# One Strassen input stored as f32 sums and split at its use, and low parts moved to VectorE, in a one-core hybrid decoder step

## What is computed

```python
(c_q, c_kv, k_r, z_mla, conv_b, conv_c, conv_h, z_conv,
 q_x, z_x, gates) = split(h @ w_in)                 # w_in: 1024 x (672 + 512*7 + 3072)
y_mla  = latent attention (prompt: causal; sample: 4,096 cached rows in pages)
y_conv = conv_b * conv3(conv_c * conv_h)
y_x    = cross-attention of 4 heads into 256 memory rows
g = sigmoid(gates)
m = (g[0] * ((y_mla  * silu(z_mla))  @ w_p_mla)
   + g[1] * ((y_conv * silu(z_conv)) @ w_p_conv)
   + g[2] * ((y_x    * silu(z_x))    @ w_p_x))
out = layer_norm(2**0.25 * h + m @ w_o)
```

## Time and profile before

| | us |
|---|---|
| runs without profile | 1522.39, 1523.32, 1525.07; median 1523.32 |
| profiled execution | 1521.78 |
| its span, first to last instruction | 1520.0 |
| busy: PE, PEld | 1429.2 (94%), 1238.8 (81%) |
| busy: DVE, ACT, POOL | 845.1 (56%), 521.1 (34%), 304.5 (20%) |
| mean granted TensorE clock | 0.955 of full |

### The profile page before, as it was taken

One profiled execution on the slowest core, in us unless ns is written; L12 is line 12 of the kernel. 1 busy time (PEld: TensorE's weight loads), 2 busy tenths in 40 slices (PEclk: granted clock), 3 DMA queues, 4 the chain that ended last, 5 costly groups with the idle time before them and its releaser, 6 DMA issues.

```text
span 1520.0 us, 28154 instructions
## 1 busy us (share of the span) xinstructions
PE 1429.2 (94%) x11192; PEld 1238.8 (81%) x11192; DVE 845.1 (56%) x1643; ACT 521.1 (34%) x1130; POOL 304.5 (20%) x225
## 2 busy tenths in 40 slices
PE   7997899999988888899899999999999999998997
PEld 7996787777755555556599999999999999998885
DVE  3476347766775334444457577664444444479645
ACT  3331346665361111223333334433333342124100
POOL 3110017666542333330100000000000003236000
PEclk9998899999998777789999999999999999999999
DMA  5465120000472434447912212123333337452522
GB/s 213 126 203 170 54 83 2 1 1 5 130 268 91 133 132 133 161 155 269 380 43 56 85 43 84 45 71 100 101 115 102 100 100 247 158 194 79 223 97 69
DMA packets 117462, 183.29 MB, mean 121 GB/s; under 512 B 14322, under 2 KB 85810, under 8 KB 115540
## 3 DMA queue, kind: packets, MB, share of 16 engines
q1 hardware_dynamic: 107092, 145.84, 29.0%
q0 software_dynamic: 10240, 35.66, 6.9%
HBM read 142.94 MB, written 38.51 MB: 119 GB/s over the span
## 4 chain that ended last, share of the span: by engine, by line
PE 49%; DVE 1%; issue 0%; ACT 0%; DVEq 0%
PE ps L2468 33%; PE ps L2499 10%; PE ps L2533 6%; PE ps L2519 0%; DVE p_ul L2713 0%; DVE p_h L2836 0%; DVE p_h L2839 0%; DVE p_slots L2643 0%; DVE p_stats L2823 0%; DVE p_h L2819 0%; PE ps L2509 0%; DVE p_mv L2830 0%; ACT p_rt L2620 0%; DVE p_rs L2834 0%; DVE p_stats L2828 0%
## 5 line engine op out<-in xcount | busy, mean ns | idle before, releaser
L2468 PE MATMUL ps<-p_x,p_w 128*128 128x272 f32 x4032 | 506.5, 289 | 0.9 <-PEq L2004 0.9
L2468 PEld LDWEIGHTS ps<-p_x,p_w 128*128 128x128 f32 x4032 | 506.3, 188 | 1.0 <-issue 1.0
L1937 POOL TENSOR_TENSOR p_w<-p_wr,p_w 128x512 fp32r<-128x512 f32 x25 | 39.9, 1598 | 645.6 <-ACT p_w L1929 645.6
L1546 PE MATMUL ps<-p_kT,p_q_rows 32*64 32x256 f32 x2048 | 127.5, 503 | 30.2 <-issue 24.6
L2499 PE MATMUL ps<-p_uh,p_w 128*128 128x352 f32 (+1 forms) x576 | 146.4, 334 | 9.0 <-issue 6.2
L1016 POOL TENSOR_SCALAR p_pr<-p_pr,p_rec 128x896 f32<-128x896 f32 (+3 forms) x64 | 109.8, 1725 | 158.6 <-DVE p_rec L980 158.0
L1546 PEld LDWEIGHTS ps<-p_kT,p_q_rows 32*64 32x64 f32 x2048 | 73.1, 172 | 75.9 <-issue 68.4
L2727 DVE TENSOR_TENSOR p_w<-p_sum,p_w 128x512 fp32r<-128x512 f32 x94 | 65.0, 691 | 120.0 <-ACT p_w L1929 120.0
L2499 PEld LDWEIGHTS ps<-p_uh,p_w 128*128 128x128 f32 x576 | 104.6, 193 | 10.7 <-issue 10.7
L1929 ACT ACTIVATE p_w<-p_wr 128x512 fp32r<-128x512 f32 x96 | 60.1, 626 | 141.2 <-PE ps L2499 82.1
L1714 DVE CUSTOM_DVE_ANT_0 p_sc<-ps,p_zero 128x256 f32<-128x256 f32 x64 | 23.4, 421 | 137.9 <-PE ps L1553 87.1
(11 more groups left out here) (338 smaller groups left out, 2584.4 us busy)
## 6 DMA issues: line engine op xcount, KB each, us to landing
p_wr<-w_in SPq DMA_DIRECT2D x48, 512.0 KB, 3.6
g_kept<-p_slots SPq DMA_DIRECT2D x48, 272.0 KB, 2.5
p_x<-t_kept SPq DMA_DIRECT2D x8, 1088.0 KB, 10.0
p_ring<-g_kept SPq DMA_DIRECT2D x16, 544.0 KB, 4.3
p_x<-x_kept SPq DMA_DIRECT2D x6, 1088.0 KB, 7.9
t_kept<-p_t_high SPq DMA_DIRECT2D x16, 272.0 KB, 2.4
t_kept<-p_t_low SPq DMA_DIRECT2D x16, 272.0 KB, 3.1
p_gy<-g_kept SPq DMA_DIRECT2D x8, 544.0 KB, 5.7
```

Of the source, the lines that this page charges most:

```text
L1546: pe.matmul(cols(i, f), q_rows[rows, b % 2, d, :], kT[rows, x:x + S, 2 * f:2 * f + 2, d, :], start=(d == 0), stop=False, tile_position=(32 ...
L2468: last = pe.matmul(ps[:, lo + z, 0:PW], w[:, q % NW, part, t, :], v[:, t, z * PW:(z + 1) * PW], start=(i in STARTS and t == 0 and n == 0), ...
```

## The change

In the first stage the x sums are no longer split. VectorE makes a part in one of eight buffers, and SyncE stores the f32 part once (16 stores instead of 32). Six of the twelve `b_store` calls move into the loop in which x comes in; the other six stand between the later t stores. `high` and `lower` are gone.

The HBM copy of T1 to T4 is one block each, loaded into the place of the low part: ten x loads instead of 14, five of them in decode_attention (B11 twice, T1, T2, B21's high) and five in cross_decode. Two new functions split a block in place: ScalarE copies 128x2176 into the high part (`split_high`), VectorE subtracts (`split_low`). T1 and T2 are split in cross_decode's rounds 4 to 7, T3 and T4 in Strassen group 0.

In the merge, every low part from q = 3 on is made by VectorE, also those of the projections and of w_o. The four `u_low` of branch 0 stand within the last Strassen group. Branches 1 and 2 multiply piece by piece, but add, copy and subtract whole rows of 1,088 columns, in two row buffers.

```diff
-    SETS = 4
+    SETS = 8
...
-        return (n % 2, n // 2) if n < NGR // 2 else (2 + n % 2, (n - NGR // 2) // 2)
+        return (n % 4, n // 4) if n < NGR // 2 else (4 + n % 4, (n - NGR // 2) // 4)
...
+            def t_store(n):
+                z, _ = t_set(n)
+                kt, pp, cols = t_place(n)
+                cols = slice(pp * PW + cols.start, pp * PW + cols.stop)
+                sp.wait_ge(t_step, 4 * (n + 1))
+                sp.dma_start(k["t_kept"][:, :, kt, cols].rearrange("b p w -> p b w"), t_raw[z][:, :, :]
+                             ).then_inc(t_out[z], 16)
...
+                tiles = -((2 * pp + th + 1) * -PW // P)
+                sp.wait_ge((xh_done, xl_done)[part], tiles)
...
+                if 5 <= i < 8:
+                    b_store(4 * (i - 5))
+                    b_store(4 * (i - 5) + 2)
...
+            for n in range(4):
+                t_store(n)
...
+            for n in range(4, NGR // 2):
                 t_store(n)
-                if n - 2 < 12:
-                    b_store(n - 2)
+            for n in range(1, 12, 2):
+                b_store(n)
+                if n >= 5:
+                    t_store((NGR + n - 5) // 2)
+            for n in range(NGR // 2 + 4, NGR):
+                t_store(n)
...
-                    if g < NGR // 2:
-                        high(NGR // 2 + g)
...
-X_EARLY = [(B11, 0), (B11, 1), (T1, 0), (T1, 1), (T2, 0), (T2, 1), (B21, 0), (B21, 1), (T3, 0)]
+X_EARLY = [(B11, 0), (B11, 1), (T1, 1), (T2, 1), (B21, 0)]
+X_PARTS = ((B11, T1, T2), (B21, T3), (B22, T4))
...
+def split_high(nc, act, e, n):
+    blk = T_ORDER[n]
+    hi, lo = e["x"][blk]
+    act.wait_ge(e["x_in"][blk], e["x_all"][blk])
+    nc.scalar.activation(hi[:, :, :], f32(lo[:, :, :]), ACT.Copy).then_inc(e["t_high"], 1)
...
+def split_low(dve, e, n):
+    hi, lo = e["x"][T_ORDER[n]]
+    dve.wait_ge(e["t_high"], n + 1)
+    dve.tensor_tensor(lo[:, :, :], f32(lo[:, :, :]), f32(hi[:, :, :]), ALU.subtract).then_inc(e["t_low"], 1)
...
+                if r in (4, 6):
+                    split_high(nc, act, e, (r - 4) // 2)
...
+                if r in (5, 7):
+                    split_low(dve, e, (r - 5) // 2)
...
+                    if g == 0 and i == 3:
+                        split_high(nc, act, e, 3)
-                    if g == NGRP - 1 and i in (3, 4):
-                        u_high(0, 2 * (i - 3))
-                        u_high(0, 2 * (i - 3) + 1)
+                    if g == NGRP - 1 and i in (2, 3):
+                        u_high(0, 2 * (i - 2))
+                        u_high(0, 2 * (i - 2) + 1)
...
+                    w_o_high(d)
+                    act.wait_ge(zed, d + 1)
+                    nc.scalar.activation(mh[:, d, :], stage[:, d % 2, :], ACT.Copy).then_inc(mh_done, 1)
...
-            for q in (*range(1, NW), *range(NQ1, NQ)):
+            for q in range(1, NW):
                 w_low(nc, pool, e, q)
-                if NQ - 6 <= q < NQ - 2:
-                    for t in range(2):
-                        w_o_low(2 * (q - NQ + 6) + t)
...
+                if g == 0:
+                    split_low(dve, e, 2)
...
                 add(g, 0)
+                if g == 0:
+                    split_low(dve, e, 3)
                 lower(q + A12)
+                if g == NGRP - 1:
+                    u_low(0, 0)
+                    u_low(0, 1)
                 add(g, 1)
                 lower(q + S3)
+                if g == NGRP - 1:
+                    u_low(0, 2)
+                    u_low(0, 3)
...
-            for j in range(4):
-                u_low(0, j)
...
                     dve.tensor_tensor(z, src, gate, ALU.mult).then_inc(freed, 1)
+                    if bi == 2 and n == 0 and d:
+                        m_low(d - 1)
+                if bi:
+                    dve.wait_ge(freed, NP * (p + 1))
+                    dst, z = mt[:, d, :], stage[:, d % 2, :]
                     if bi == 1:
                         dve.tensor_tensor(dst, dst, z, ALU.add).then_inc(summed, 1)
+                    else:
+                        dve.wait_ge(summed, d + 1)
+                        dve.tensor_tensor(z, z, dst, ALU.add).then_inc(zed, 1)
...
+                lower(NQ1 + p + NW)
+                if bi == 2:
+                    w_o_low(d)
+            m_low(KT - 1)
```

More of the change, by code:

```diff
@@ L128, in project_latents @@
     tok, kr = k["tok"], k["kr"]
-    SETS = 4
+    SETS = 8
     size = 4 * 4 * GW
[L132 to L138, removed]
+    places = [at - (4 - z) * size for z in range(4)] + [k["qkv_at"] + z * size for z in range(3)] + [k["w_end"]]
+    t_raw = [Map(nc, where)(f"p1_t_raw{z}", [P, 4, GW]) for z, where in enumerate(places)]
     assert k["qkv_at"] + 3 * size <= w_at + 8 * KT * LAT and k["w_end"] + size <= k["top"] - 4 * 3 * P
@@ L357, in _ @@
                     if h == 1 and n == 0:
-                        for z in range(2):
-                            act.wait_ge(t_out[z], 32 * NGR // 4)
+                        for z in range(4):
+                            act.wait_ge(t_out[z], 32)
                     pn = min(tn, SEQ - t0)
@@ L431, in _ @@
                         make(n)
-                    for n in (2 * (i - 5), 2 * (i - 5) + 1):
-                        lower(n)
             dve.wait_ge(squared, 2 * NT)
@@ L1428, in late_space @@
                   for part in range(2)] for blk in range(7)]
-    first = k["sem"]("p7_x_first")
-    late["x_in"] = {blk: first for blk in X_FIRST} | {blk: k["sem"](f"p7_x_in{blk}") for blk in (T3, B22, T4)}
+    x_in = [k["sem"](f"p7_x_in{z}") for z in range(3)]
+    late["x_in"] = {blk: x_in[z] for z, part in enumerate(X_PARTS) for blk in part}
+    late["x_all"] = {blk: 16 * sum(1 if b in T_ORDER else 2 for b in part) for part in X_PARTS for blk in part}
+    late["t_high"], late["t_low"] = k["sem"]("p7_t_high"), k["sem"]("p7_t_low")
     def x_free(blk, part):
@@ L2205, in merge @@
     raw_o = slabs("p8_raw_o", ring_at[:2], [P, D])
-    stage = Map(nc, e["rest_at"])("p7_stage", [P, ST, PIECES[0][1]])
-    slab_at = [e["rest_at"] + 4 * ST * PIECES[0][1] + 4 * T * d for d in range(5)] + [e["slab_at"]] + ring_at[2:]
+    stage = Map(nc, e["rest_at"])("p7_stage", [P, 2, T])
+    slab_at = [e["rest_at"] + 4 * T * d for d in range(2, 7)] + [e["slab_at"]] + ring_at[2:]
     assert slab_at[4] + 4 * T <= x_at
@@ L2580, in _ @@
             w_high(nc, act, e, 2)
+            split_high(nc, act, e, 2)
             for g in range(NGRP):
@@ L2714, in u_low, with w_o_low, m_low @@
                                   ).then_inc(ul_done, 1)
[L2716 to L2720 removed]
+            def w_o_low(t):
+                dve.wait_ge(oh_done, t + 1)
+                if t == 0:
+                    dve.wait_ge(ul_done, 12)
+                dve.tensor_tensor(ol[t][:, :], raw_o[t % 2][:, :], f32(oh[t][:, :]), ALU.subtract).then_inc(ol_done, 1)
+            def m_low(d):
+                dve.wait_ge(mh_done, d + 1)
+                dve.tensor_tensor(ml[d][:, :], stage[:, d % 2, :], f32(mh[:, d, :]), ALU.subtract).then_inc(ml_done, 1)
             def lower(q):
[L2723 removed]
+                if NW <= q < NQ:
                     dve.wait_ge(w_hi, q + 1)
@@ L2761, in _ @@
                 finish(g, 1)
[L2762 to L2763 removed]
+                if g == NGRP - 1:
+                    lower(q + A22)
             for p in range(NJ):
```

132 lines of the change are left out of this document (33 added, 99 removed).

## The result

The changed kernel took **1484.42 us** (median of 4 runs, 1482.75 to 1488.75) against 1524.19 us for the kernel before, measured beside it (4 runs, 1522.39 to 1525.81). The ratio is 0.9744, 95% interval 0.9719 to 0.9768. The forecast was 1485.6 us, range 1480 to 1495. The profiled execution took 1485.23 us with a span of 1483.4, so the span fell by 36.6 us where the sum said 37.7.

What follows compares the result with a forecast made beforehand. TensorE was taken to set the time almost alone from 751.58 us, with removable waits elsewhere. Terms -20.1 - 1.5 - 2.6 + 0.5 - 6.2 - 7.8 = -37.7 took 1521.78 to 1484.1; 1.5 for the median gave 1485.6 us, range 1480 to 1495.

Steps and rivals of the forecast that it cites:

- First stage: Start to the next stage's first transpose: without splits TensorE no longer waits in the qx loop, ending at 134.0; -20.1 us.
- Clock behind it: Stretch from the next stage's first transpose to the prompt's scores: -1.5 us.
- cross_decode: Fewer loads remove the 5.58 us wait and slowness behind it (-6.6); four split instructions cost 4.0; together -2.6 us.
- Strassen group 0: Splits of T3 and T4 in Strassen's first group, T4's close to late for the seventh product: +0.5 us, bounds 0 and 2.
- Start of the projections: First projections tile: with low parts made earlier it ends at 1263.8 instead of 1270.1; -6.2 us.
- third branch: Projections' third branch: 8.3 us of loss goes if VectorE keeps up, less 0.5 for what goes wrong; -7.8 us.
- turn of 7.4 us: VectorE's loop per tile in the third branch, closing through ScalarE: 7.4 us against TensorE's 5.95.
- it just holds: Third branch's end: last `m_low` done 8.4 us after the last piece, needed by the output's row tile 0 at 9.8.
- the loss is GpSimd's: Third branch before: GpSimd's 5.25 us pair of w_o low parts holds back the weight's low part TensorE needs; 8.3 us lost.
- rule of the Trainium skill: Third branch: by shared SBUF interfaces, VectorE's 2.38 us for 1,088 columns should vanish with GpSimd's work, leaving 1.28.
- rival of rows that stay at 2.38: Third branch: row operations stay at 2.38 us, the loop takes 10.6 us, total 1509 us; 3 in 100.
- late VectorE: Third branch: whole-row operations cost 1.6 us instead of 1.28, VectorE misses both margins, total 1493 us; 14 in 100.

Runs made afterwards that it cites:

- pair 2: Kernel before and changed kernel run again with the experiments, at a higher granted clock in decode: 1420.82 and 1382.29 us, ratio 0.9735.
- pair 1: The prediction's two profiled executions, kernel before against changed kernel: 1521.78 and 1485.23 us.

## Why the prediction was right, point by point

- **First stage, -20.1: measured -21.8 and -20.6.** The forecast end held: qx ends at 133.0 (134.0 forecast), VectorE is done at 123.8. Of the 6.1 us laid on the lower clock in the qx loop before, the clock explains 5.1 at most (10.2 us at 0.50); where the last 1.0 went is open. Named as causes were ScalarE's link and the two-part reuse of buffers; the runs with both put back show that neither is needed once the split is out of the loop and the stores are fewer and placed otherwise. Cause in part mistaken, size right.
- **Clock behind it, -1.5: measured -2.2 and -1.9.** Within the bounds; the gap is 0.9 us, not 1.7. But in four of the twelve profiles with the changed first stage the stretch took 61.4 us (before: 62.1 and 61.7), with 3.4 us at half clock. The term is a matter of the execution, and both pairs had the lucky one.
- **cross_decode, -2.6: measured -3.0 and -4.3.** The wait's part was priced at 6.6; from the kernel before to the one without splits it is 32.0 - 24.0 = 8.0, and putting the loads back cost 8.7. The prediction names 5.58 for the wait, 0.93 for the slow turn behind it and 1.0 for other work, and its 6.6 has room for only one of the last two. The splits were priced at 4.0 and cost 3.3. The wait is shown to be the loads'. The bounds (-3.8 to -0.3) miss pair 2 by 0.5.
- **Strassen group 0, +0.5: measured +2.6 and +0.6.** This is the mis-sized term of pair 1. T4's split costs the 0.35 us gap, as the margin said; the 2 us more are a half clock at Strassen's start, for which the sum had no term.
- **Between the prompt's scores and cross_decode, 0: measured +2.1 and +1.1.** The change doesn't touch this stretch; no cause was sought.
- **Start of the projections, -6.2, and third branch, -7.8: measured -6.0 and -8.4 by tile** (-4.8 and -7.0 in pair 2, where the kernel before lost less to the clock). The turn of 7.4 us was measured at 7.38. The last `m_low` was forecast 8.4 us behind the last piece with the need at 9.8. It came at 9.6, and the need was at about 9.5, because the first row tile starts at 1378.35, 0.16 us before the last piece ends. So "it just holds" missed, by the 0.2 us of the output. The step "the loss is GpSimd's" is half shown: GpSimd's pair is what TensorE waited for, yet GpSimd can do the same work without loss, one part in a turn.
- **The rule of the Trainium skill** (GPSIMD Engine Reference, Specifications: shared SBUF interfaces, contention for a VectorE instruction with two SBUF inputs) agrees with 1.28 to 1.29 us rows in the changed kernel and 1.84 to 2.05 with GpSimd back, while the PSUM product stays at 0.515. The rival of rows that stay at 2.38 is out.
- **The late VectorE** (14 in 100, 1493) did not come, but nothing was left of the margin of 1.4 us that the forecast had.
- **The total, 1485.6 against 1484.42, owes something to luck.** The first two stretches gained 2.4 us more than forecast, cross_decode and the projections 0.4 more each, against +2.1 before cross_decode, 2.1 of half clock in Strassen and 0.2 in the output. And the 1.5 us added for the median above the profiled execution had the wrong sign: the profiled execution took 1485.23, above the median.

## What to carry to other kernels

When a change bundles several cures for one wait, put each back alone: here the eight buffers, the cut link, the whole rows and the move off GpSimd could each be undone at no cost. Price a loop through two engines by its busy time and the round trips that stay open in it: whole rows saved busy time and made the turn 0.5 us longer. Work that moves to a later stage is cheapest where its engine idles and nothing that TensorE needs next stands behind it; the splits cost 3.3 us in the rounds, and one of them ahead of a weight made a wait of 2.0 us out of one of 0.7.

## What the runs showed of the hardware

- **One kernel, two levels of decode.** Whether it is the chip or the occasion is open: all three chips of the experiments had the higher clock. In pair 1 the changed kernel's 2,048 key matmuls of 32 rows in decode took 547 ns in the median at a granted clock of 0.76 to 0.88, in the experiments 374 at 0.97 to 1.00, and the stretch that they stand in was 98 us shorter, of 102 us of the whole kernel. Ratios between kernels stayed (0.9744 and 0.9735); differences in us must not be taken across.
- **The half clock is not a property of the code alone.** The same instructions had it at Strassen's start in three executions of seven, for about 2 us, and behind the first stage in four of twelve, for 1.5 us.
- **Contention goes both ways.** GpSimd's subtraction of 512 columns took 1.26 us alone and 2.18 on average beside VectorE's two-input rows; VectorE's 1,088 columns went from 1.28 to 3.50 at the most:

```profile
1248.90 2.24 DVE L2715 TENSOR_TENSOR p_ml<-p_stage,p_mh 128x1088 fp32r<-128x1088 f32 x1 [0.46 <-ACT p_mh L2599]
1249.94 2.35 POOL L1924 TENSOR_TENSOR p_w<-p_wr,p_w 128x512 fp32r<-128x512 f32 x1
1252.25 2.41 POOL L2616 TENSOR_TENSOR p_ol<-p_raw_o,p_oh 128x1024 fp32r<-128x1024 f32 x1
1252.30 3.50 DVE L2799 TENSOR_TENSOR p_stage<-p_stage,p_mt 128x1088 f32<-128x1088 f32 x1
```

These rows look like turns and not like shared speed: whichever starts second ends about one undisturbed length behind the other's end. GpSimd's weight: 1248.90 + 2.24 + 1.26 = 1252.40, recorded end 1252.29. VectorE's row: 1252.25 + 2.41 + 1.28 = 1255.94, recorded end 1255.80. The kernel before fits as well: there GpSimd's weight ends at 1258.15, and the `p_ul` row begun at 1256.91 takes 2.38 us and ends at 1259.29, 1.14 behind it.
